# Query tiles searched in pairs: the even tile's threshold on VectorE, the odd tile's by sign sums on ScalarE with GpSimd

## What is computed

```python
def indexer_scores(q_idx, w_idx, k_idx, valid):            # 8 indexer heads
    dots = jnp.einsum("bqhd,bld->bqhl", q_idx, k_idx) * (IDX_DIM ** -0.5)
    s = jnp.einsum("bqh,bqhl->bql", w_idx * (N_IDX_HEADS ** -0.5), jax.nn.relu(dots))
    return jnp.where(valid, s, -jnp.inf)
...
scores = indexer_scores(qib, wb, k_idx, valid)             # per block of 128 queries
_, sel = lax.top_k(scores, 256)                            # 256 keys of each query
att = attend_selected(qb, k_sel, v_sel, sel <= tb)         # softmax over these, 8 heads, 2 K/V heads
...
mo = mem_attend(z["q_mem"], mk, mv)                        # 4 heads over 256 memory tokens
o = concat([att * silu(g_att), conv * silu(g_conv), mo * silu(g_mem)]) @ w_out
y = x + rms_norm(o, g_post)
```

## Time and profile before

| | us |
|---|---|
| three runs, median (lowest to highest) | 2663.28 (2654.77 to 2669.16) |
| the profiled execution, own time | 2667.36 |
| its span in the trace | 2665.6 |
| PE busy, share | 2195.9, 82% |
| DVE busy, share | 1812.5, 68% |
| ACT busy, share | 756.4, 28% |
| POOL busy, share | 129.5, 5% |

### The profile page before, as it was taken

One profiled execution on the slowest core, in us unless ns is written; L12 is line 12 of the kernel. 1 busy time (PEld: TensorE's weight loads), 2 busy tenths in 40 slices (PEclk: granted clock), 3 DMA queues, 4 the chain that ended last, 5 costly groups with the idle time before them and its releaser, 6 DMA issues.

```text
span 2665.6 us, 34212 instructions
## 1 busy us (share of the span) xinstructions
PE 2195.9 (82%) x12640; PEld 1736.0 (65%) x12640; DVE 1812.5 (68%) x4093; ACT 756.4 (28%) x1415; POOL 129.5 (5%) x174
## 2 busy tenths in 40 slices
...
DMA packets 53609, 121.79 MB, mean 46 GB/s; under 512 B 12944, under 2 KB 25912, under 8 KB 52448
## 3 DMA queue, kind: packets, MB, share of 16 engines
...
## 4 chain that ended last, share of the span: by engine, by line
PE 47%; DVE 36%; issue 10%; ACT 3%; DMA 1%; POOL 1%; PEld 1%; SPq 1%; DVEq 0%; ACTq 0%; POOLq 0%; PEldq 0%
DVE sb_junk L916 12%; PE psum L563 12%; PE psum L596 9%; PE psum L1137 6%; DVE sb_sc L901 5%; PE psum L1129 4%; DVE sb_p L935 3%; PE psum L1148 3%; PE psum L1106 3%; PE psum L1119 2%; DVE sb_g L952 2%; DVE sb_c L958 1%; PE psum L611 1%; PE psum L1579 1%; DVE sb_sc L1067 1%
## 5 line engine op out<-in xcount | busy, mean ns | idle before, releaser
L916 DVE TENSOR_SCALAR_CACHE_REDUCE sb_junk<-sb_sc,sb_c 128x384 bf16<-128x384 f32 (+13 forms) x434 | 641.0, 1477 | 11.9 <-DVE sb_mix L1050 2.4
L563 PE MATMUL psum<-sb_w,sb_xt 128*128 128x512 f32 (+5 forms) x1088 | 324.8, 459 | 0.5 <-DVE sb_xt L377 0.5
L1119 PE MATMUL psum<-sb_ks,sb_qa 128*128 128x512 f32 (+3 forms) x640 | 196.6, 442 | 136.5 <-ACT sb_p L855 105.9
L1137 PE MATMUL psum<-sb_v,sb_ptb 128*128 128x64 f32 x2176 | 303.3, 284 | 6.6 <-ACT sb_ptb L821 5.4
L1137 PEld LDWEIGHTS psum<-sb_v,sb_ptb 128*128 128x128 f32 x2176 | 291.0, 206 | 16.4 <-ACT sb_ptb L821 15.3
L1129 PE MATMUL psum<-sb_con,sb_p 128*128 128x128 f32 x1280 | 235.4, 312 | 63.2 <-ACT sb_p L863 41.4
L821 ACT ACTIVATE sb_ptb<-psum 128x512 f32<-128x512 f32 (+3 forms) x352 | 188.2, 539 | 304.8 <-PE psum L1129 304.5
L563 PEld LDWEIGHTS psum<-sb_w,sb_xt 128*128 128x128 f32 (+1 forms) x1088 | 178.5, 185 | 134.6 <-issue 125.1
L1106 PEld LDWEIGHTS psum<-sb_qa,sb_w 128*128 128x128 f32 x2048 | 252.1, 196 | 20.0 <-DMA sb_w<-in_w_in 7.2
L1106 PE MATMUL psum<-sb_qa,sb_w 128*128 128x128 f32 x2048 | 256.5, 280 | 6.6 <-DMA sb_w<-in_w_in 5.1
L1095 PE MATMUL psum<-sb_ks,sb_qi 128*128 128x512 f32 (+3 forms) x608 | 187.7, 437 | 85.4 <-ACT sb_r L833 75.3
...
## 6 DMA issues: line engine op xcount, KB each, us to landing
qt_s<-sb_qt SPq DMA_DIRECT2D x32, 512.0 KB, 2.7
sb_x<-in_x_prompt SPq DMA_DIRECT2D x16, 512.0 KB, 3.8
xt_s<-sb_xt SPq DMA_DIRECT2D x16, 512.0 KB, 2.6
sb_qa<-xt_s SPq DMA_DIRECT2D x16, 512.0 KB, 3.3
sb_qa<-qt_s SPq DMA_DIRECT2D x16, 512.0 KB, 3.3
sb_xres<-in_x_prompt SPq DMA_DIRECT2D x16, 512.0 KB, 5.0
out_y_prompt<-sb_y SPq DMA_DIRECT2D x16, 512.0 KB, 3.0
sb_qi<-qt_s SPq DMA_DIRECT2D x14, 512.0 KB, 5.8
```

Of the source, the lines that this page charges most:

```text
L563: mm = pe.matmul(out, m.xt[:, p, k, 0:n], m.w1[:, k, lo:hi], start=(k == 0), stop=(k == KD - 1))
L916: return dve.tensor_scalar(m.junk[:, 0:w], m.sc[:, i % 2, 0:w], m.c[:], 0.0, ALU.is_ge, ALU.add, accum_out=m.cnt[:])
L1119: mm = pe.matmul(m.score2(slot)[:, lo:lo + n], m.qa[:, h, :], m.ks[:, 2 * kv + x, c[0] + lo:c[0] + lo + n], start=(x == 0), stop=(x == 1))
L1137: mm = pe.matmul(o, m.ptb[:, g, x * P:(x + 1) * P], v, start=st, stop=sp)
```

## The change

Stage B searches tiles in pairs. In steps 2n and 2n+1 the even tile 2n+2 is searched on DVE (15 passes in the even step, 16 in the odd), and the odd tile 2n+3 on ACT and POOL, with as many passes. Index scores run four tiles ahead instead of two (`AHEAD`), in two steps more ahead of step 0 (j = -2 and -1, for tiles 2 and 3), and `sc` has four slots of the widths needed. Room for them comes from `ks`, now three blocks with the high part over the low one; the query tile is loaded a second time with its halves exchanged, in two more DMAs (`load_q`).

```diff
@@ b_sync
+    def load_q(q, half, i, sem):
+        flat = [q[:, x, :, :].rearrange("p h n -> p (h n)").bitcast(F32) for x in range(2)]
+        sp.dma_start(flat[0], io.qt_s[half, i]).then_inc(sem, 16)
+        sp.dma_start(flat[1][0:HD, :], io.qt_s[half, i, HD:P, :]).then_inc(sem, 16)
+        sp.dma_start(flat[1][HD:P, :], io.qt_s[half, i, 0:HD, :]).then_inc(sem, 16)
...
+    for i in range(FIRST + 1, AHEAD + 1):
+        load_idx(i)
@@ b_pool
+    def candidate(n, it):
+        seen, own = n * BITS + it + 1, n * (2 * BITS + 1) + 2 * it
+        step = m.part("step").bitcast(I32)
+        pool.wait_ge(s.a_cand, n * (BITS + 1) + it + 1)
+        pool.tensor_tensor(m.am[:], m.an[:], step[:, it:it + 1], ALU.subtract).then_inc(s.a_pool, 1)
+        pool.wait_ge(s.a_cnt, seen)
+        pool.tensor_scalar(m.ag[:], m.acnt[:], m.thr[:, n % 2:n % 2 + 1], float(2 ** (BITS - 1 - it)), ALU.is_ge,
+                           ALU.mult).then_inc(s.a_pool, 1)
+        pool.wait_ge(s.a_pool, own + 2)
+        pool.tensor_tensor(m.an[:], m.am[:], m.ag[:], ALU.add).then_inc(s.a_cand, 1)
@@ b_act
+    def probe(j, it):
+        n, i = j // 2, j // 2 * 2 + 3
+        act.wait_ge(s.a_cand, n * (BITS + 1) + it + 1)
+        act.activation(m.ajunk[:, 0:width(i)], m.sc(i), ACT.Sign, bias=m.an[:].bitcast(F32),
+                       scale=2.0 ** SHIFT, accum_out=m.acnt[:]).then_inc(s.a_cnt, 1)
...
+                    if hp % 2 == 1 and its:
+                        probe(j, its[done])
...
+            if done < upto:
+                probe(j, its[done])
+                done += 1
             for c in chunks(w, 512):
                 take_group(("t", j, h, c))
+            for it in its[done:upto]:
+                probe(j, it)
@@ b_vector
+    def exact(i):
+        n, y = i // 2 - 1, slice(i % 4, i % 4 + 1)
+        dve.wait_ge(s.a_fin, n + 1)
+        ac, after = m.ac[:].bitcast(F32), m.anext[:].bitcast(F32)
+        ch.inc(dve.tensor_tensor(m.ulp[:], after, ac, ALU.subtract))
+        ch.link(count(i, m.anext.bitcast(F32)))
+        ch.link(dve.tensor_scalar(m.cnt[:], m.cnt[:], m.k[:, y], None, ALU.is_ge))
+        ch.link(dve.scalar_tensor_tensor(out=m.cf[:], in0=m.ulp[:], scalar=m.cnt[:], in1=ac, op0=ALU.mult, op1=ALU.add))
+        dve.sem_inc(s.a_used, 1)
...
+        if searched(j + AHEAD):
+            for c in chunks(width(j + AHEAD), 512):
+                for h in range(0, NIH, 3):
+                    if done < upto:
+                        search(d, done, (j + AHEAD, c), h)
...
+                if j >= 1 and c[0] == 0:
+                    normalise(j - 1)
...
+        if j % 2 == 0 and n >= 1:
+            exact(2 * n + 1)
+            select(2 * n + 1, m.cf)
...
+            if h in (4, 5) and j % 2 == 1 and n < NPAIR - 2:
+                prepare(2 * n + 5 if h == 4 else 2 * n + 4)
+        if d is not None and j % 2 == 1:
+            select(d, m.c)
@@ b_tensor
-                    mm = pe.matmul(m.score2(slot)[:, lo:lo + n], m.qa[:, h, :],
-                                   m.ks[:, 2 * kv + x, c[0] + lo:c[0] + lo + n], start=(x == 0), stop=(x == 1))
+                    mm = pe.matmul(m.score2(slot)[:, lo:lo + n], m.qa[:, x, h, :],
+                                   m.ks[:, kv, c[0] + lo:c[0] + lo + n], start=(x == 0), stop=(x == 1))
```

More of the change, by code:

```diff
@@ L99 @@
     ("causal", 128),
+    ("step", 32),
     ], [
@@ L804, in b_pool @@
         pool.tensor_tensor(m.y[:], m.y[:], m.xres[:], ALU.add).then_inc(s.y_sum, 1)
+    for j in range(NT):
+        if j >= 1:
+            y_scale(j - 1)
+        n = j // 2
+        if n < NPAIR - 1:
+            if j % 2 == 0:
+                first_candidate(n)
+            its = probes(j)
+            for x, it in enumerate(its):
+                candidate(n, it)
+                if x == Y_AFTER and j >= 1:
+                    y_add(j - 1)
+            if j % 2 == 1:
+                last_candidate(n)
+        else:
+            y_add(j - 1)
+    pool.wait_ge(s.s_last, NT)
+    gather_pages(pool, m, s, io, range(4))
+    y_scale(NT - 1)
+    y_add(NT - 1)
 def b_act(act, m, s):
@@ L821, in take_group @@
         act.activation(m.ptb[:, g, 0:cols], m.turn[slot][:, 0:cols], ACT.Copy).then_inc(s.t_act, 1)
-    for i in STEPS:
-        j = i - 1
-        if indexed(i + 1):
-            for c in chunks(width(i + 1), 512):
+    def probe(j, it):
[3 more added lines that the diff above has]
+                       scale=2.0 ** SHIFT, accum_out=m.acnt[:]).then_inc(s.a_cnt, 1)
+    for j in range(FIRST - AHEAD, NT):
+        its = probes(j)
+        done = 0
+        if searched(j + AHEAD):
+            for c in chunks(width(j + AHEAD), 512):
                 for hp in range(4):
-                    slot, n, _, count = scores.of[("D", i + 1, c, hp)]
+                    slot, n, _, count = scores.of[("D", j + AHEAD, c, hp)]
                     act.wait_ge(s.s_done, n)
@@ L850, in b_act @@
         act.activation(m.gate[:], m.gate[:], ACT.Exp, scale=-1.0).then_inc(s.zln, 1)
+        if its:
+            probe(j, its[done])
+            done += 1
         slot = scores.of[("M", j)][0]
@@ L859, in b_act @@
             take_group(("tm", j, x))
+        start = done
         for h in range(NH):
             w = width(j)
+            upto = start + (len(its) - start) * (h + 1) // NH
             act.wait_ge(s.nb, NH * j + h + 1)
```

280 lines of the change are left out of this document (158 added, 122 removed).

## The result

The changed kernel takes **2716.5 us** (median of four runs, 2712.4 to 2724.3) against 2666.2 for the kernel before beside it (2654.8 to 2669.9): a ratio of 1.02, 95% interval 1.016 to 1.024. The prediction said 2700, slower. The profiled execution took 2714.8 us, its span is 2712.7 (before 2665.6).

The account below looks back on a forecast made before the run. DVE bounds preludes (step start to memory exponents), PE the attention heads. Terms -9 + 43 + 25 + 18 + 22 - 64 = +35 on 2667.4 give 2702, median 2698, rounded up to 2700 us; range 2620 to 2790.

Parts of the forecast that it names:

- Stage A and step 0: Kernel start: half the key transposes save 9 us; tile 3's late queries and ten sums in step 0 cost 43.
- Steps 1 to 3: Stage B: gate blocks bound preludes, and two thirds of the sign sums' time in the short heads shows, +25 us.
- Steps 4 to 7: Stage B: preludes 155 us, heads 173, projections 59, together 387 against 369.1 before, +18 us.
- 34 sums at 0.2 to 0.4 us add 10: Heads of steps 4 to 7: sign sums on ACT add 10 us to 157 us of heads without search.
- gap that a probe opens: PE's work, whole kernel: interruptions by sign sums lower its granted clock; forecast rounded up from 2698 to 2700 us.
- Steps 8 to 11: Stage B: preludes 230 us, heads 238, projections 59, together 527 against 504.9 before, +22 us.
- Steps 12 to 15: Stage B: without index scores, preludes 101 us, heads 312, projections 61, together 474 against 537.5 before, -64 us.
- The two prices of a sum: Heads: behind an exponent its length less 1.15 us, ahead its whole length; 8.3 and 13 to 15 us per step 12, 13.
- Second copies of the attention queries: Stage B: two more DMAs each on SP land while PE waits for the memory exponents, costing 0 us.
- Rival two: Heads: about 130 sign sums each wait 0.8 us more for POOL under DVE's two-input operations, 2805 us; chance 0.17.
- Rival one: Heads: sums fall into ACT's waits and PE keeps its cadence, so about 105 us of penalties go, 2595 us; chance 0.25.
- Rival three: First steps: tile 3's load is served beside the weights and short heads hide half their sums, 2655 us; chance 0.13.

Follow-up runs that it names:

- narrow sums: The changed kernel with every ACT sign sum over 128 of its tile's keys, work left out and thresholds wrong: 2636.3 us.
- the early load: The changed kernel with the indexer queries of tiles 3 and 4 issued ahead of the output weight: 2700.5 us.
- the kernel before with narrow counts: The kernel before with DVE's counts of odd tiles over 128 keys, work left out and thresholds wrong: 2546.5 us, ratio 0.958.

## Why the prediction was right, point by point

- **Stage A and step 0, right in sum.** PE's last work of stage A ended 7.2 us earlier (9 said), tile 3's scores began at 714.85 (720 said), step 0's own at 727.85 (735). The ten sums in its heads cost 3.0 us there, not 11: that term was too large.
- **Steps 1 to 3, right sum, wrong split.** 25.9 us, but the heads show 106.1 us with wide and 98.7 with narrow sums, so some 7 of it are the sums' width where I had 25 for the sums alone. The preludes grew by 9.4 (27.0 + 31.2 + 29.2 against 78.0), where I had called them bounded by the gate blocks. The heads grew by 14.6 in all, so about 7 more have no cause that the runs show. That the total came out is luck.
- **Steps 4 to 7, the step that failed**: +44.6 against +18. The preludes came to 165.0 us (155 said) and the heads to 186.1 (173 said), projections to 62.6 (59). The term "34 sums at 0.2 to 0.4 us add 10" was not it: narrow sums left the heads where they were, in sum. What I lacked is PE's clock: 0.78 over these steps against 0.90, so that equal matmuls took longer (34.91 for 29.82 us in step 5's heads). Of the 44.6 us PE's idle time has 4.0 and its busy time 40.6 (337.72 for 297.12 in the stretches); 9.6 of these are 33 more matmuls of index scores, some 31 the same matmuls at the lower clock. In the heads alone PE even idled less than before, 30.0 us for 36.8. The prediction had 2 us for this "gap that a probe opens", in the whole kernel.
- **Steps 8 to 11, right.** Preludes 57.7, 51.7, 64.2 and 56.1, sum 229.7 (230 said; step 10 was worked out as 65.6); heads 232.2 (238 said). Moving the selection confirmed its place on the path, step by step.
- **Steps 12 to 15, right in number, half right in cause.** Preludes 31.4, 21.9, 22.3, 19.9 (34, 22, 25, 20 said); heads 86.8, 92.2, 68.1 and 71.0 (83, 89, 68, 72 said). The two prices of a sum, behind an exponent and ahead of one, come to 43 us; taking the sums' width away gave 46.4. But the prices were worked out as waits of PE, and the waits give 24.9; the other 21.5 are PE's lower clock, which the working had at nothing. That the two together come near 43 is luck. The sum itself took 1.99 us and 0.19, as the exponent in the earlier trace rows.
- **Second copies of the attention queries: 0 was too low.** PE waited 29.4 us for these loads, where it had waited 12.6. Its products with the values waited 29.9 us for ACT's copies, where they had waited 5.4; in the heads a sum now often stands ahead of the copies. Waits in stage B of the kernel before and then after (total us, times, longest):

```profile
PE psum L1119 <- DMA sb_qa<-qt_s: 12.6, 8, 2.3
...
PE psum L1137 <- ACT sb_ptb L821: 5.4, 16, 0.5
```

```profile
PE psum L1262 <- ACT sb_ptb L892: 29.9, 54, 4.7
PE psum L1244 <- DMA sb_qa<-qt_s: 29.4, 8, 4.0
...
ACT sb_ajunk L898 <- POOL sb_an L826: 9.8, 14, 3.9
```

- **Rival two (the candidate comes late) fell**: ACT waited 9.8 us for POOL in 217 sums. The bare round on POOL is 0.69 us; 0.7 was taken. DVE does block POOL, but briefly: under the scan of 3.44 us shown above POOL's subtraction took 3.11 where it takes 0.19 alone, under an accumulate its addition took 0.62; under the counts and the masks these two kept to 0.19 (timeline of DVE and POOL, then POOL in the scan):

```profile
1708.00 0.75 DVE L996 SCALAR_TENSOR_TENSOR sb_sc<-sb_r,sb_widx,sb_sc 128x512 f32<-128x512 f32 x1
1708.17 0.62 POOL L826 TENSOR_TENSOR sb_an<-sb_am,sb_ag 128x1 int32<-128x1 int32 x1
```

```profile
1756.74 3.11 POOL L821 TENSOR_TENSOR sb_am<-sb_an,sb_con 128x1 int32<-128x1 int32 x1
```

  The Trainium skill ("GPSIMD Engine Reference", § Specifications) names two SBUF inputs of a VectorE instruction as a case of contention, and these rows agree: scan and accumulate have two, count one. The rival failed on the duration, since accumulates last 0.75 us and stand in preludes, where ACT has time.
- **Rival one (ACT has room)** is half right: in steps 4 to 7 it holds as far as one profile of each kernel can tell, in 12 and 13 not. **Rival three** fell with tile 3's scores, which came at 715 and not before 710; the early load brings 9.6 us of it.
- **The decode stage, -12.0, was not forecast and isn't the change's.** In the execution of the kernel before the chain has a gap that no other profile shows, and the kernel before with narrow counts, whose decode stage is the same, goes straight on. Whether the other executions of the kernel before have this gap isn't recorded. The first fence is before, the second that kernel:

```profile
2607.24 3.77 PE psum L1682 x16
2611.01 11.29 issue
2622.30 7.00 PE psum L1688 x32
```

```profile
2495.39 3.79 PE psum L1683 x16
2499.85 7.00 PE psum L1689 x32
```

So two errors partly cancel: stage B ended 59 us later where 35 were said, and 12 us come back because the forecast was added to the very execution that had the gap.

**Open:** which idle stretch of PE sets off the clock's falls. In steps 4 to 7 it isn't the sums' width, in 12 and 13 the clock rose when the width went, and filling one gap moved the falls without removing time. That the waits for the second query copies cost what they show wasn't tried, nor the overhang of `select` in odd steps by itself.
